# The last LayerNorm of a mixture-of-experts block: three engines instead of one

## The reference

```python
h_lat = layer_norm(DN_ALPHA * h_lat + mod_lat[5] * ffn_lat, ln_g[l, 1], ln_b[l, 1])

def layer_norm(x, g, b):
    xf = x.astype(F32)
    mu = jnp.mean(xf, -1, keepdims=True)
    var = jnp.mean(jnp.square(xf - mu), -1, keepdims=True)
    return ((xf - mu) * lax.rsqrt(var + LN_EPS) * g.astype(F32) + b.astype(F32)).astype(x.dtype)
```

## Time and profile before

| | |
|---|---|
| median of 3 runs | 3078.07 us (3077.36 to 3081.32) |
| time of the profiled execution | 3083.48 us |
| its span (first to last record) | 3081.9 us |
| busy share of the span | PE 90%, DVE 53%, ACT 29%, POOL 12% |
| the stage `stage_combine` in it | from 3013.8 us to the end |

### The profile page before, as it was taken

How to read it: one execution, slowest core, us unless ns; L and a number is a source line. 1 busy time by engine, 2 the same in 40 slices (tenths; PEclk the granted TensorE clock), 3 DMA queues, 4 the chain that set the end, 5 groups by cost and what they waited for, 6 DMA issues and landing times. The chain is left out here.

```text
span 3081.9 us, 32474 instructions
## 1 busy us (share of the span) xinstructions
PE 2764.0 (90%) x12416; PEld 2054.2 (67%) x12416; DVE 1634.6 (53%) x1533; ACT 903.1 (29%) x1033; POOL 355.7 (12%) x236
## 2 busy tenths in 40 slices
PE   7889899888999779999986799999885999999994
PEld 4444684333888667787875677877445888888871
DVE  4624335463333046534328744242457888888876
ACT  2403231000333214331000010000003777777760
POOL 1300000000000032000023230000000212221120
PEclk9889999998999879999998899999996999999997
DMA  6432113222123232121110011111434999999955
GB/s 206 144 130 111 40 41 120 82 92 69 45 91 114 91 106 80 57 69 45 46 47 34 28 38 41 48 42 64 167 157 152 364 365 365 362 361 385 391 205 232
DMA packets 90423, 433.23 MB, mean 141 GB/s; under 512 B 15651, under 2 KB 25139, under 8 KB 75544
## 3 DMA queue, kind: packets, MB, share of 16 engines
q1 hardware_dynamic: 68952, 372.49, 33.0%
q0 software_dynamic: 21376, 59.42, 5.3%
HBM read 399.40 MB, written 53.42 MB: 147 GB/s over the span
## 5 line engine op out<-in xcount | busy, mean ns | idle before, releaser
L335 PE MATMUL ps<-uT_upper_rest,ring_rest 128*128 128x512 f32 x1360 | 542.9, 399 | 0.0
L335 PEld LDWEIGHTS ps<-uT_upper_rest,ring_rest 128*128 128x128 f32 x1360 | 259.7, 191 | 61.9
L335 PE MATMUL ps<-uT_upper_rest,cs_upper 128*128 128x512 f32 x320 | 129.0, 403 | 55.0 <-DVE cs_val L1960 46.8
L2348 PE MATMUL ps<-ex_u_raw_rest,uT_rest 128*128 128x256 f32 x560 | 156.6, 280 | 0.0
L335 PE MATMUL ps<-uT_upper_rest,xbc_upper 128*128 128x512 f32 x336 | 135.4, 403 | 6.1 <-DVE ring_rest L726 6.1
L1733 PE MATMUL ps<-sb_merged,ring 128*128 x256 | 115.9, 616 | 26.2 <-DVE sb_merged L1808 26.2
L2346 PE MATMUL ps<-ring_rest,uT_rest 128*128 128x256 f32 (+1 forms) x416 | 135.3, 325 | 3.2 <-DVE uT_rest L2612 2.4
L2346 PE MATMUL ps<-ex_upper,uT_rest 128*128 128x256 f32 (+1 forms) x424 | 136.3, 322 | 0.0
L2347 PE MATMUL ps<-ex_upper,uT_rest 128*128 128x256 f32 (+1 forms) x424 | 134.7, 318 | 0.0
L335 PE MATMUL ps<-uT_rest,xbc_upper 128*128 128x512 f32 x336 | 133.3, 397 | 0.0
L2347 PE MATMUL ps<-ring_rest,uT_rest 128*128 128x256 f32 (+1 forms) x416 | 133.1, 320 | 0.0
(11 more groups left out here) (451 smaller groups left out, 6312.6 us busy)
## 6 DMA issues: line engine op xcount, KB each, us to landing
sb_spare<-in_ex_g SPq DMA_DIRECT2D x35, 2048.0 KB
ex_u_raw<-in_ex_u SPq DMA_DIRECT2D x35, 2048.0 KB, 10.5
sb_merged<-in_ex_d SPq DMA_DIRECT2D x35, 2048.0 KB, 9.3
ring<-in_w_mod SPq DMA_DIRECT2D x48, 512.0 KB, 4.2
ring<-in_w_gate SPq DMA_DIRECT2D x32, 512.0 KB, 3.2
ring<-in_dft SPq DMA_DIRECT2D x24, 512.0 KB, 3.2
ring<-in_w_ssd SPq DMA_DIRECT2D x21, 512.0 KB, 3.2
spectra<-fs_spec POOLq DMA_DIRECT2D x8, 1024.0 KB, 4.2
```

Of the source, the lines that this page charges most:

```text
L335: last = self.nc.tensor.matmul(out, weight, x[:, k, lo:hi], start=(k == 0 and n == 0), stop=(k == kt - 1 and n == 2))
L2348: return nc.tensor.matmul(out, left_up, w_lo, start=False, stop=last)
```

## The change

The combine stage's norm is divided among three engines, and DVE's work for neighbouring tiles is interleaved.

- **ACT** takes the statistics: a Copy of the row with scale -1/D that also gives its sum (`accum_out`), which is minus the mean; a Square with that as bias, whose sum is D times the variance; the root as before; and a third pass, Identity with scale 1/root and bias -mean/root, which writes the normalised row into `normed` (two buffers).
- **DVE** keeps the two operations that make `s` (now the function `residual`), does three operations on single columns (`variance`: x 1/D + EPS; `normalise`: reciprocal, and -mean x 1/root), and multiplies `normed` with `ln_g` (`gain`). `bn_stats`, `bn_aggr` and both full-row `scalar_tensor_tensor` of the norm are gone. `residual(t + 1)` stands ahead of `variance(t)`, and `gain(t - 1)` between `variance(t)` and `normalise(t)`. `residual(t + 1)` overwrites the buffer of tile t - 1, so it waits for ACT's third pass over that tile (`centre_ready`).
- **POOL** adds `ln_b` to each row of `res`; SP's store waits for that.
- **`ln_g` and `ln_b`** are loaded in the experts' stage, into slots 5 and 6 of `k.uT`, behind the first two blocks' loads on SP's queue and ahead of the later blocks' loops. The first set of `y` gets a buffer of its own (`cb_y0`), and PE waits for the diagonals tile by tile.

```diff
@@ stage_experts, SP
+                sp.wait_ge(u_turned, TT)
+                sp.wait_ge(u_out, 16 * TT)
+                sp.dma_start(k.uT[:, 5, :], k.row("ln_g2")).then_inc(early_in, 16)
+                sp.dma_start(k.uT[:, 6, :], k.row("ln_b2")).then_inc(early_in, 16)
                 with sp.Fori(1, EXPERTS // 2) as j:
@@ stage_combine
-        y, h1 = (k.uT, k.spare), merged[:, :, :]
+        y, h1 = (sb("y0", [P, TT, D]), k.spare), merged[:, :, :]
+        ln_g, ln_b = k.uT[:, 5, :], k.uT[:, 6, :]
@@ SP
-                load(0)
-                sp.dma_start(ln_g[:, :], k.row("ln_g2")).then_inc(small_in, 16)
-                sp.dma_start(ln_b[:, :], k.row("ln_b2")).then_inc(small_in, 16)
-                for t in range(1, TT):
-                    load(t)
@@ PE
-                pe.wait_ge(diag_set, 2 * TT)
                 for t in range(TT):
+                    pe.wait_ge(diag_set, 2 * (t + 1))
@@ ACT
                 for t in range(TT):
+                    acc = s[:, t % 2, :]
+                    act.wait_ge(summed, t + 1)
+                    nc.scalar.activation(centred[:, :], acc, ACT.Copy, scale=-1.0 / D,
+                                         accum_out=total[:, t:t + 1]).then_inc(act_own, 1)
+                    act.wait_ge(act_own, t + 1)
+                    nc.scalar.activation(centred[:, :], acc, ACT.Square, bias=total[:, t:t + 1],
+                                         accum_out=spread[:, t:t + 1]).then_inc(spread_in, 1)
                     act.wait_ge(var_ready, t + 1)
-                    nc.scalar.activation(rstd[:, :], mv[:, 1:2], ACT.Sqrt).then_inc(root, 1)
+                    nc.scalar.activation(rstd[:, t:t + 1], spread[:, t:t + 1], ACT.Sqrt).then_inc(root, 1)
+                    act.wait_ge(inverse, 2 * t + 2)
+                    if t >= 2:
+                        act.wait_ge(scaled, t - 1)
+                    nc.scalar.activation(normed[:, t % 2, :], acc, ACT.Identity, scale=rstd[:, t:t + 1],
+                                         bias=total[:, t:t + 1]).then_inc(centre_ready, 1)
+
+            @block.gpsimd
+            def _(pool):
+                for t in range(TT):
+                    pool.wait_ge(scaled, t + 1)
+                    nc.gpsimd.tensor_tensor(res[:, t % RING, :], res[:, t % RING, :], ln_b, ALU.add).then_inc(ready, 1)
@@ DVE
-                    stt(out=res[:, t % RING, :], in0=acc, scalar=rstd[:, 0:1], in1=ln_b[:, :],
-                        op0=ALU.mult, op1=ALU.add).then_inc(ready, 1)
+                def variance(t):
+
+                    v.wait_ge(spread_in, t + 1)
+                    nc.vector.tensor_scalar(spread[:, t:t + 1], spread[:, t:t + 1], 1.0 / D, EPS, ALU.mult,
+                                            ALU.add).then_inc(var_ready, 1)
+
+                def normalise(t):
+
+                    v.wait_ge(root, t + 1)
+                    nc.vector.reciprocal(rstd[:, t:t + 1], rstd[:, t:t + 1]).then_inc(inverse, 1)
+                    v.wait_ge(inverse, 2 * t + 1)
+                    nc.vector.tensor_tensor(total[:, t:t + 1], total[:, t:t + 1], rstd[:, t:t + 1],
+                                            ALU.mult).then_inc(inverse, 1)
+
+                def gain(t):
+
+                    v.wait_ge(centre_ready, t + 1)
...
+                    nc.vector.tensor_tensor(res[:, t % RING, :], normed[:, t % 2, :], ln_g, ALU.mult).then_inc(scaled, 1)
+
+                residual(0)
+                for t in range(TT):
+                    if t + 1 < TT:
+                        if t:
+                            v.wait_ge(centre_ready, t)
+                        residual(t + 1)
+                    variance(t)
+                    if t:
+                        gain(t - 1)
+                    normalise(t)
+                gain(TT - 1)
```

More of the change, by code:

```diff
@@ L2081, in tail_stages, with stage_experts @@
         plan = sb("plan", [1, EXTRA + 1], I32)
-        stage_experts(k, rows, rows_at, weights, plan, merged, merged_rest)
-        stage_combine(k, rows, weights, merged)
-def stage_experts(k, rows, rows_at, weights, plan, merged, merged_rest):
+        early_in = ctx.enter_context(k.nc.semaphore("early_in"))
+        stage_experts(k, rows, rows_at, weights, plan, merged, merged_rest, early_in)
+        stage_combine(k, rows, weights, merged, early_in)
+def stage_experts(k, rows, rows_at, weights, plan, merged, merged_rest, early_in):
     nc, a, ps = k.nc, k.a, k.ps
@@ L2626, in _, with stage_combine @@
                 extra_blocks(v, body)
-def stage_combine(k, rows, weights, merged):
+def stage_combine(k, rows, weights, merged, early_in):
     nc, a, ps = k.nc, k.a, k.ps
     with k.stage("cb") as (sb, sem):
-        y, h1 = (k.uT, k.spare), merged[:, :, :]
+        y, h1 = (sb("y0", [P, TT, D]), k.spare), merged[:, :, :]
+        ln_g, ln_b = k.uT[:, 5, :], k.uT[:, 6, :]
         diag = sb("diag", [P, 2, TT, P])
-        ln_g, ln_b = sb("ln_g", [P, D]), sb("ln_b", [P, D])
         s, res = sb("s", [P, 2, D]), sb("res", [P, RING, D])
-        stats, mv, rstd = sb("stats", [P, 2, 6]), sb("mv", [P, 2]), sb("rstd", [P, 1])
-        small_in, y_in, h_in = sem("small_in"), [sem(f"y_in{t}") for t in range(TT)], [sem(f"h_in{t}") for t in range(TT)]
+        centred, normed = k.uT[:, 7:8, :].rearrange("p k t -> p (k t)"), sb("normed", [P, 2, D])
+        total, spread, rstd = sb("total", [P, TT]), sb("spread", [P, TT]), sb("rstd", [P, TT])
+        y_in, h_in = [sem(f"y_in{t}") for t in range(TT)], [sem(f"h_in{t}") for t in range(TT)]
         out = [sem(f"out{n}") for n in range(RING)]
-        dve, diag_set, mixed, mix_read, var_ready, root, ready = (sem(n) for n in (
-            "dve", "diag_set", "mixed", "mix_read", "var_ready", "root", "ready"))
+        diag_set, mixed, mix_read, summed, act_own, spread_in, var_ready, root, inverse, scaled, ready = (sem(n) for n in (
+            "diag_set", "mixed", "mix_read", "summed", "act_own", "spread_in", "var_ready", "root", "inverse", "scaled",
+            "ready"))
+        centre_ready = sem("centre_ready")
         def banks(t):
@@ L2649, in _ @@
             def _(sp):
-                def load(t):
+                for t in range(TT):
                     for r in range(2):
@@ L2685, in _, with residual @@
                 for t in range(TT):
-                    act.wait_ge(var_ready, t + 1)
-                    nc.scalar.activation(rstd[:, :], mv[:, 1:2], ACT.Sqrt).then_inc(root, 1)
+                    acc = s[:, t % 2, :]
[5 more added lines that the diff above has]
+                                         accum_out=spread[:, t:t + 1]).then_inc(spread_in, 1)
+                    act.wait_ge(var_ready, t + 1)
+                    nc.scalar.activation(rstd[:, t:t + 1], spread[:, t:t + 1], ACT.Sqrt).then_inc(root, 1)
[9 more added lines that the diff above has]
+                    nc.gpsimd.tensor_tensor(res[:, t % RING, :], res[:, t % RING, :], ln_b, ALU.add).then_inc(ready, 1)
             @block.vector
             def _(v):
-                ch = Chain(v, dve)
                 stt = nc.vector.scalar_tensor_tensor
-                for t in range(TT):
+                def residual(t):
                     acc = s[:, t % 2, :]
@@ L2698, in _ @@
                     v.wait_ge(h_in[t], 16)
[L2699 to L2706, removed]
@@ L2707, in _ @@
-                    if t == 0:
[L2708 to L2712, removed]
+                    stt(out=acc, in0=h1[:, t, :], scalar=ALPHA, in1=acc, op0=ALU.mult, op1=ALU.add).then_inc(summed, 1)
+                def variance(t):
+                    v.wait_ge(spread_in, t + 1)
+                    nc.vector.tensor_scalar(spread[:, t:t + 1], spread[:, t:t + 1], 1.0 / D, EPS, ALU.mult,
+                                            ALU.add).then_inc(var_ready, 1)
@@ new lines, in normalise @@
+                def normalise(t):
[6 more added lines that the diff above has]
+                    v.wait_ge(centre_ready, t + 1)
+                    if t == 0:
+                        v.wait_ge(early_in, 32)
```

## The result

The changed kernel takes 3094.34 us (median of 6 runs, 3089.57 to 3096.28), the kernel before 3078.88 beside it (6 runs, 3077.36 to 3081.32). The ratio is 1.0048, with an interval of 1.0036 to 1.006: slower by 11 to 18 us. The forecast was 3073.3, with a range to 3082; what came is its rival "slower", which had 0.14 and a time of 3090.9.

The account below looks back on a forecast made before the run. DVE's own stream was taken to bound the last stage. Start, seven turns of 5.3 us and tail gave a span of 3077.1 instead of 3081.9, 4.8 us saved; from the median 3078.07 that is 3073.3 us, range 3069 to 3082.

Parts of the forecast that it names:

- slower: Last stage: column product loses to POOL's add and waits 2.5 us in each of seven turns; 3090.9 us, chance 0.14.
- It wins by 0.18 us: In `normalise`, the column product starts 0.18 us before POOL's add and so is not stopped by it.
- The 0.10 from `gain` to the product: On DVE, the column product of `normalise` starts 0.10 us after `gain` ends.
- The 0.28 from `gain` to POOL: POOL's add of `ln_b` starts 0.28 us after `gain` ends, from an earlier row's hop from ACT to POOL.
- the price is 17.6 us: Total of DVE's waits for POOL's add, 2.5 us in each of seven turns, if the column product loses.
- The turn: One tile's cycle through DVE and ACT in the last stage: 5.24 us lower bound, 5.7 upper, 5.3 taken.
- ACT's passes: Last stage on ACT: Copy with sum 1.06 us, Square 1.15, each plus 0.19 for the accumulator read; third pass 1.24.
- The two branches tie: In a turn, ACT's two statistics passes take 2.4 us with overlaps beside DVE's `residual` at 2.50; ACT adds 0 to 0.2.
- The early rows: `ln_g` and `ln_b` loaded in the experts cost nothing there; `residual(1)` starts at 3028.0 instead of 3031.04.
- The sum: Whole last stage, start, seven turns and tail: span 3077.1 us instead of 3081.9, 4.8 us saved.
- holds for DVE operations that read two SBUF tensors: DVE beside POOL: whoever comes first wins; in a turn it concerns `residual`'s second pass, `gain` and the column product.

Follow-up runs that it names:

- POOL held back: Changed kernel plus a memset of 8 scratch columns on POOL, and a wait on it, ahead of each add; ratio 0.9985 to the kernel before.
- the third buffer: Kernel with the column product as tensor_scalar, given three buffers of `s` so `residual(t + 1)` waits for tile t - 2's third pass; one run, 3072.9 us.
- pattern: Changed kernel with POOL's add written as a four-dimensional view (4 x 4 x 64) of the same rows; stage 67.4 us.
- second wait: Changed kernel with one more wait ahead of POOL's add, for its own last add, long done; stage 67.4 us.
- loop: Changed kernel with POOL's adds in a hardware loop of two rounds of four, each waiting for a value from the register; stage 67.4 us.
- product first: Changed kernel with `normalise(t)` placed ahead of `gain(t - 1)` on DVE; ratio 0.9979 to the kernel before.
- one input: Changed kernel with `normalise`'s column product as a tensor_scalar, one tensor input and a pointer scalar; ratio 0.9987 to the kernel before.
- the early rows alone: Kernel before with only `ln_g` and `ln_b` loaded during the experts and a separate buffer for the first `y`; ratio 0.9995.
- the two engines: Changed kernel without POOL's add, ACT's third pass, `gain` and the column product; DVE does the norm in two full-row passes; ratio 0.9965 to the kernel before.

## Why the prediction was wrong

**The step that failed** is the sentence "It wins by 0.18 us" in the part on DVE beside POOL. Both numbers behind it were from rows. The 0.10 from `gain` to the product was right (0.10). The 0.28 from `gain` to POOL was not: it measured 0.08. The difference changed sign, from 0.18 ahead to 0.02 behind, and with it the whole case. The mechanism, its place and the point from which it decides ("less than 0.10 us after `gain`") stood in the text as the rival; the mistake was to give the rival 0.14 on the strength of one row, which it itself called one "from ACT to POOL, not from DVE". Where the price is 17.6 us and the gain 4.8, and the hops between DVE and ACT are 0.03 to 0.04, the order of two instructions due within 0.2 us of each other should have been close to even.

**The other steps held**, which can be seen where the race is taken away:

- The turn. The sum's lower bound, 5.24, is what the kernel with POOL held back shows (5.26), and in the changed kernel 7.42 - 2.18 = 5.24. The forecast used 5.3; the overlaps of the earlier trace rows hold throughout.
- ACT's passes: 1.04 and 1.15 us with reads of 0.19, third pass 1.24, `gain` 1.22, POOL's add 2.34. Each within 0.02 of its row.
- The two branches tie: shown by the third buffer.
- The early rows: 3.0 us for tile 1, nothing in the experts.
- The sum, 52.9 us of stage with 4.8 saved: 53.3 and 4.4 saved with POOL held back, and 4.6 us by the ratio 0.9985 (its interval, 0.9971 to 0.9999, reaches from 0.3 to 9). For that kernel the forecast would have been right.

One reading was too narrow, though it changed nothing here: that the stop "holds for DVE operations that read two SBUF tensors". The kernel before has it for one, beside the very add of the earlier trace rows, which ran from 57.34 to 61.99:

```profile
57.54 4.53 DVE L507 COPY ft_hid_t<-ft_hid 64x128 f32 x1
```

```profile
L507 DVE COPY ft_hid_t<-ft_hid x8: 219/4524/4526, 41.6 to 150.8; 64x128 f32 x8
```

A small copy with one input takes 0.22 us once, with POOL idle, and 4.52 to 4.53 the seven times that it is issued 0.2 us into POOL's add, and ends 0.08 us after it.

**The size of the rival.** It was given as 70.5 us of stage (52.9 + 17.6) and measured 67.4. A blocked turn costs 2.18, not 2.5 (2.2 us over seven turns): the add ends 0.2 us earlier, as it starts at 0.08 and not at 0.28, and the product ends with it and not a product's length behind it; the turn itself is 5.24 and not 5.3 (0.4); and tile 1 follows tile 0 by 3.43 and not 3.8 (0.4). 70.5 less these three is 67.5.

**What isn't settled.** The medians differ by 15.5 us (11.1 by the lower end of the interval), the stage by 9.7. In the two profiles another 1.5 us lies between the first `y` load and DVE's first pass (11.9 against 10.4), which the last section has; but that part takes either value in kernels of all kinds. Ahead of that load the changed kernel's profile is 1.0 us shorter, and 9.7 + 1.5 - 1.0 is all of the 10.2 by which the two profiled spans differ. The rest of the 15.5 is in runs without a profile. It may be scatter: single runs of the three kernels with the same stage (pattern, second wait, loop) took 2.0 less, 6.5 more and 7.1 more than a single run of the kernel before beside them.

## What to carry to other kernels

When work is moved to POOL, list every DVE instruction that is due near POOL's start and reads two tensors of SBUF, the one-column ones first, and the copies from SBUF to SBUF too: length is no protection, a product of 128 numbers waited 2.2 us and a copy of 128 columns 4.3. Where the order rests on a margin of tenths of a microsecond, don't forecast the order but take the race away: give the small operation its second number as a pointer (0.21 us in each of seven turns beside POOL's add). That is shown for one column only. Over a full row the same form was held up in the kernel before, beside the POOL product that starts at 1749.83 and ends at 1751.72:

```profile
1750.81 1.47 DVE L1988 TENSOR_SCALAR cs_conv<-cs_line,sb_cols 128x1024 f32<-128x1024 f32 x1
```

Two of that line's four lie beside POOL's products and take 1.47 and 1.23; the other two, with POOL idle, take 0.75. And when a stage is bound by one engine, a ring through three engines may end no faster than that engine alone with its statistics taken off it (5.31 against 5.17 us a turn, and a tail shorter by 7 us).

## What the runs showed of the hardware

- A DVE pass stopped by a POOL instruction has less than its full time left when POOL ends: with POOL's add ending at 3035.90 (product first) and 3062.48 (one input), the full-row passes ended 1.09 and 1.08 us later, though each takes 1.22 to 1.23 alone.
- The stop isn't confined to two inputs: a one-input copy of 64x128 took 4.53 us instead of 0.22 beside POOL's add, and a full-row `tensor_scalar` 1.47 instead of 0.75 beside POOL's product. A one-column `tensor_scalar` with a pointer was not stopped (0.21).
- A margin of 0.02 us decides and is stable: the product lost in seven of seven turns in the changed kernel.
- PE starts the stage at the lower of its two clock levels, 1.2 GHz (granted clock 0.50), after waiting 20 us for data. When it rises to 2.4 GHz differs between executions. Tile 0's two groups of four matmuls, and a window that lies in the second (busy time by engine, granted clock, DMA share, GB/s), in the changed kernel:

```profile
3017.95 3.75 PE L2677 MATMUL ps<-cb_y,cb_diag 128*128 128x512 f32 x4 [20.58 <-DMA sb_spare<-y_rows]
3021.50 3.17 PE L2677 MATMUL ps<-sb_spare,cb_diag 128*128 128x512 f32 x4
```

```profile
3022.00:3024.00 2.00, 2.00 (x3) 0.68 (x2) 0.00 (x0) 0.00 (x0) 0.00 (x0) 0.50 1.04 418
```

and in the kernel with the one-input product:

```profile
3011.26 3.35 PE L2677 MATMUL ps<-cb_y,cb_diag 128*128 128x512 f32 x4 [20.45 <-DMA sb_spare<-y_rows]
3014.44 1.88 PE L2677 MATMUL ps<-sb_spare,cb_diag 128*128 128x512 f32 x4
```

```profile
3014.00:3016.00 2.00, 2.00 (x6) 0.96 (x5) 0.00 (x0) 0.00 (x0) 0.00 (x0) 0.98 1.02 410
```

The same work took 6.7 us in the one and 5.1 in the other. The fourteen profiles fall into two halves by it: the second group of four takes 2.98 to 3.20 us in seven and 1.88 in the other seven. So DVE's first pass starts 11.6 to 12.0 us behind the first `y` load in the first seven (the changed kernel, the early rows alone and the two engines among them) and 9.8 to 10.4 in the others (the kernel before, the one-input product and the loop on POOL among them). No edit goes with it. A stage compared from its first DMA would have carried these 1.5 us; the stage as measured here doesn't.
